# Twelve modulation tiles moved from the attention stage to later normalizations, in a two-layer hybrid decoder trunk

## The reference, cut to what matters

```
for i in range(2):
    mod = silu(c) @ ada_w[i] + ada_b[i]            # 6 sections of 1024
    sh_a, sc_a, g_a, sh_f, sc_f, g_f = split(mod, 6)
    h = rmsnorm(x, norm_mix[i]) * (1 + sc_a) + sh_a
    y = diff_attention(h) if i == 0 else retention(h)
    x = x + g_a * y
    h = rmsnorm(x, norm_ffn[i]) * (1 + sc_f) + sh_f
    x = x + g_f * moe(h)                           # 64 experts, 8 of them for a token
out = rmsnorm(x, final_norm)
```

## Time and profile before

| | us |
|---|---|
| median of 3 runs | 1436.48 (1433.49 to 1436.8) |
| the profiled execution | 1434.63 |
| its span, first to last instruction | 1432.9 |

### The profile page before, as it was taken

The page is one execution under the profiler, slowest core; times in us unless marked ns, Lnnn a source line. Parts: engine busy times, 40 slices in busy tenths (PEclk is TensorE's granted clock), DMA queues, the critical chain, the costliest instruction groups (busy, mean ns, idle before and its releaser), DMA issues.

```text
span 1432.9 us, 32974 instructions
## 1 busy us (share of the span) xinstructions
PE 1327.3 (93%) x12029; PEld 876.8 (61%) x12030; DVE 550.7 (38%) x1226; ACT 446.3 (31%) x885; POOL 207.0 (14%) x663
## 2 busy tenths in 40 slices
PE   4999789999999999998799999799999999999996
PEld 2878566555555555554499998665555555555553
DVE  2556565332223323232533455553332323322333
ACT  3443452222222222221444454522222222222222
POOL 8200102111111111111000000011111111111110
PEclk9999999999999999999899999899999999999998
DMA  9999995999999999999995434449999999999994
GB/s 352 350 382 398 407 368 209 422 420 422 421 422 423 421 421 422 423 421 421 377 290 185 168 118 147 162 175 421 421 421 421 422 421 422 422 422 421 422 422 199
DMA packets 113338, 516.06 MB, mean 360 GB/s; under 512 B 9632, under 2 KB 46624, under 8 KB 63360
## 3 DMA queue, kind: packets, MB, share of 16 engines
q1 hardware_dynamic: 109920, 509.64, 88.8%
q0 software_dynamic: 2656, 3.49, 0.9%
q10 hardware_dynamic: 704, 2.10, 0.4%
HBM read 514.10 MB, written 1.09 MB: 360 GB/s over the span
## 4 chain that ended last, share of the span: by engine, by line
PE 71%; DMA 9%; DVE 5%; SPq 5%; ACT 5%; issue 3%; POOL 1%; ACTq 1%; DVEq 0%; POOLq 0%
PE bank L933 18%; PE bank L1115 15%; PE bank L1118 8%; PE bank L1136 8%; PE bank L1050 6%; DMA ring<-in_exp_w_dram 6%; PE bank L1091 5%; PE bank L1142 4%; SPq L346 3%; DMA ring<-in_da_w_in_dram 2%; PE bank L908 2%; DVE arena L1573 1%; ACT arena L711 1%; PE bank L1125 1%; SPq L349 1%
## 5 line engine op out<-in xcount | busy, mean ns | idle before, releaser
L1115 PE MATMUL bank<-ring,arena 128*64 128x512 f32 x768 | 176.9, 600 | 11.4 <-DMA ring<-in_exp_w_dram 11.4
L1091 PEld LDWEIGHTS bank<-arena 128*128 128x128 bf16 x3264 | 142.1, 98 | 55.5 <-issue 55.0
L1050 PE MATMUL bank<-arena_r 128*128 128x512 f32 x560 | 161.3, 418 | 3.0 <-DVE arena_r L1585 3.0
L1585 DVE TENSOR_TENSOR arena_r<-bank,arena_r 128x512 fp32r<-128x512 f32 x136 | 94.1, 692 | 154.1 <-ACT arena_r L723 154.1
L1091 PE MATMUL bank<-arena 128*128 128x64 bf16 (+1 forms) x3264 | 151.8, 207 | 0.0
L716 ACT ACTIVATE arena<-bank 128x256 f32<-128x256 f32 (+1 forms) x68 | 22.6, 333 | 387.3 <-PE bank L1115 270.1
L723 ACT CAST arena_r<-bank 128x512 fp32r<-128x512 f32 x136 | 79.7, 586 | 189.4 <-PE bank L1136 124.8
L1050 PEld LDWEIGHTS bank<-arena_r 128*128 128x128 f32 x560 | 94.6, 188 | 60.2 <-issue 47.4
L542 POOL TENSOR_TENSOR arena<-arena,pass_base 128x2 f32 x136 | 23.6, 197 | 741.6 <-PE bank L1102 727.6
L933 PE MATMUL bank<-HH_r,ring_r 128*128 128x256 f32 x448 | 128.4, 287 | 0.0
L1115 PEld LDWEIGHTS bank<-ring,arena 128*64 128x64 f32 x768 | 56.0, 138 | 111.7 <-issue 111.1
(11 more groups left out here) (273 smaller groups left out, 2154.9 us busy)
## 6 DMA issues: line engine op xcount, KB each, us to landing
ring<-in_exp_w_dram SPq DMA_DIRECT2D x264, 1024.0 KB, 23.9
ring<-in_ada_w_dram SPq DMA_DIRECT2D x48, 1024.0 KB, 13.3
HH<-in_exp_w_dram SPq DMA_DIRECT2D x40, 1024.0 KB, 20.4
mods<-in_exp_w_dram SPq DMA_DIRECT2D x40, 1024.0 KB, 24.3
arena<-in_exp_w_dram SPq DMA_DIRECT2D x40, 1024.0 KB, 25.0
ring<-in_ret_w_in_dram SPq DMA_DIRECT2D x24, 1024.0 KB, 11.9
ring<-in_da_w_in_dram SPq DMA_DIRECT2D x12, 1024.0 KB, 17.2
ring<-in_ret_w_out_dram SPq DMA_DIRECT2D x8, 1024.0 KB, 4.9
```

The costliest lines, as they stand in the source:

```text
L1050: ins = nc.tensor.matmul(banks[4 + NH * tc + hf][:, :], S[:, P * tc:P * tc + P], y[:, r, 512 * hf:512 * hf + 512], start=False, stop=(last ...
L1091: ins = nc.tensor.matmul(banks[2 - 2 * half][:, P * kk:P * kk + 2 * W], parts[:, tc, r, P * (4 * half + kk):P * (4 * half + kk + 1)], Pg[: ...
L1115: ins = nc.tensor.matmul(banks[1][W * i:W * i + W, :], xg[:, k, W * i:W * i + W], w13[j][:, k, :, :], start=(k == 0), stop=(k == KD - 1))
L1585: nc.vector.tensor_tensor(y[:, 1, 512 * hf:512 * hf + 512], banks[hf][:, :], y[:, 0, 512 * hf:512 * hf + 512], ALU.subtract).then_inc(u[f" ...
```

## The change

Sections (1, 2), (1, 3) and (1, 5) are no longer made in the attention stage, which keeps three of its six in the loop and three in its tail. (1, 2) and (1, 3) are made between the first expert loop and the second layer's first transposes, (1, 5) during its second normalization; their bias rows are loaded to other places, later. The root is taken per block of tokens, with mean and epsilon in its scale and bias. Shared tile 0 is rounded before the last output tile's wait. The first two quarters of the turned heads are evicted and rounded before output tile 1 is.

The core of the diff (left out: places of rows in memory, semaphore names, counts that follow from the order, and places of the same edits on the fourth engine):

```
-LATER = [(0, 2), (0, 3), (0, 4)] + [(1, s) for s in range(6)] + [(0, 5)]
+LATER = [(0, 2), (0, 3), (0, 4), (1, 0), (1, 1), (1, 4), (0, 5), (1, 2), (1, 3), (1, 5)]
     for i in range(12):
         order.append(("mix_in", 0, i))
-        if i >= 3 and i % 3 < 2:
-            order += later[2 * (i // 3) - 2 + i % 3]
-    order += sum(later[6:9], [])
-    order += [("mix_out", 0, i) for i in range(4)] + later[9]
+        if i >= 3 and i % 3 == 0:
+            order += later[i // 3 - 1]
+    order += sum(later[3:6], [])
+    order += [("mix_out", 0, i) for i in range(4)] + later[6]
...
     order += [("expert", 0, i) for i in range(132)]
-    order += [("mix_in", 1, i) for i in range(24)] + [("mix_out", 1, i) for i in range(8)]
+    order += later[7] + later[8]
+    order += [("mix_in", 1, i) for i in range(24)] + [("mix_out", 1, i) for i in range(8)] + later[9]

 (GpSimd)
-            store_rows(1, 0, 6, 9)
-            pool.wait_ge(rows_stored, 128)
+            store_rows(1, 0, 2, 5)
+            store_rows(1, 4, 1, 6)
+            pool.wait_ge(rows_stored, 192)
...
             for l in range(DEPTH):
+                if l == 1:
+                    store_rows(1, 5, 1, 10)
+                    pool.wait_ge(rows_stored, 384)
+                    spread(1, 5, gates_in)
...
                 if l == 0:
+                    pool.wait_ge(routed_done, 2)
+                    (four loads of the bias rows of (1, 2) and (1, 3))
                     pool.wait_ge(x_new, 4)
+                    (four loads of the bias rows of (1, 5))
+                    store_rows(1, 2, 2, 9)
+                    pool.wait_ge(rows_stored, 320)
+                    turn_mods(1, 3)
                     spread(1, 2, gate1_in)

 (ScalarE, norm_stats)
                     nc.scalar.activation(h[:, tc, :], X[:, tc, :], ACT.Square, accum_out=ss[:, tc:tc + 1]
                                          ).then_inc(sumsq, 1)
-                act.wait_ge(meansq, n + 1)
-                nc.scalar.activation(rs[:, 0:TC], ss[:, 0:TC], ACT.Sqrt).then_inc(root, 1)
+                    act.wait_ge(sumsq, TC * n + tc + 1)
+                    nc.scalar.activation(rs[:, tc:tc + 1], ss[:, tc:tc + 1], ACT.Sqrt, scale=1.0 / D, bias=eps[:, 0:1]).then_inc(root, 1)

 (ScalarE, the attention stage's tail)
             round_w("mix_out", 0, 0)
             evict_aT(15)
-            release_ada(8)
+            evict_oT(0)
+            round_oT(0)
+            release_ada(5)
             square_o(14)
+            evict_oT(1)
+            round_oT(1)
+            square_o(15)
             round_w("mix_out", 0, 1)
-            for m in range(3):
-                evict_oT(m)
-            square_o(15)
-            for m in range(3):
-                round_oT(m)
+            evict_oT(2)
+            round_oT(2)
...
-            for i in range(2, 4):
-                mixer_out(0, i)
+            mixer_out(0, 2)
+            round_w("shared", 0, 0)
+            mixer_out(0, 3)
             moe(0)
             round_w("mix_in", 1, 0)
             norm_stats()
+            release_ada(7)
+            release_ada(8)
             evict_hT()
...
+            load_root_table()
+            round_w("shared", 1, 0)
+            mixer_out(1, 7)
             moe(1)

 (TensorE)
             def moe(l):
-                if l == 0:
-                    pe.wait_ge(x_new, 1)
-                    ada(*LATER[9], ada_bank[9][:, 0:256])
+                k = (6, 9)[l]
+                pe.wait_ge(x_new, 4 * l + 1)
+                ada(*LATER[k], ada_bank[k][:, 0:256])
                 turn_h()
...
             for part in range(3):
                 ...
-                later(2 * part)
+                later(part)
                 first_half(i + 1)
                 attend(n + 1)
                 second_half(i + 1)
                 turn_a(n + 2)
-                later(2 * part + 1)
                 first_half(i + 2)
...
             moe(0)
+            ada(*LATER[7], ada_bank[7][:, 0:256])
+            pe.wait_ge(x_new, 3)
+            ada(*LATER[8], ada_bank[8][:, 0:256])
+            pe.wait_ge(bank_rows_read, 8)
             turn_h()
+            pe.wait_ge(bank_rows_read, 9)

 (VectorE)
             def norm_root(last=False):
                 n = norms[0]
-                dve.wait_ge(sumsq, TC * (n + 1))
-                nc.vector.tensor_scalar(ss[:, 0:TC], ss[:, 0:TC], 1.0 / D, EPS, ALU.mult, ALU.add).then_inc(meansq, 1)
-                dve.wait_ge(root, n + 1)
-                step(nc.vector.reciprocal(rs[:, 0:TC], rs[:, 0:TC]))
-
-                if not last:
-                    for tc in range(TC):
+                for tc in range(TC):
+                    if n == 2 and tc == 1:
+                        later_rows(7)
+                    dve.wait_ge(root, TC * n + tc + 1)
+                    step(nc.vector.reciprocal(rs[:, tc:tc + 1], rs[:, tc:tc + 1]))
+                    (block tc of h, or of the output in the last normalization)
...
             low_part("mix_out", 0, 0)
+            low_oT(0)
             keep_o(15)
+            low_oT(1)
             mean_squares(last_heads, DA_ITEMS)
-            for m in range(3):
-                low_oT(m)
+            low_oT(2)
...
             norm_root()
+            later_rows(8)
             low_part("mix_in", 1, 0)
             evict_hT()
```

More of the change, by code:

```diff
@@ L305, in trunk @@
             turns.append(("proj", i))
-            if i % 3 < 2:
-                turns.append(("ada", 2 * (i // 3) - 2 + i % 3))
-        turns += [("ada", k) for k in range(6, 9)]
+            if i % 3 == 0:
+                turns.append(("ada", i // 3 - 1))
+        turns += [("ada", k) for k in range(3, 6)]
         proj0_bank = {i: banks[7 * (n % 2)] for n, (kind, i) in enumerate(turns) if kind == "proj"}
@@ L467, in store_rows @@
                 pool.wait_ge(rows_ready, ready)
-                rows = browB[:, first:first + count, :] if l == 1 else row5 if first == 5 else browA[:, first - 2:first - 2 + count, :]
+                rows = (browA if (l, first) == (0, 2) else row5 if (l, first) == (0, 5) else rows23 if (l, first) == (1, 2)
+                        else row5_1 if (l, first) == (1, 5) else browB[:, first:first + count, :])
                 for q in range(4):
@@ L664, in round_rw @@
                 act.wait_ge(late_consts_in, 16 * 5)
-                act.wait_ge(rows_stored, 128)
+                act.wait_ge(rows_stored, 192)
                 nc.scalar.copy(rw_hi, rw[:, :, :]).then_inc(rw_rounded, 1)
             def moe(l):
-                if l == 1:
-                    load_root_table()
-                round_w("shared", l, 0)
                 norm_stats()
@@ L779, in _ @@
                 square_o(n)
-                release_ada(2 * part)
+                release_ada(part)
                 evict_proj0(i + 2)
@@ L783, in _ @@
                 square_o(n + 1)
-                release_ada(2 * part + 1)
                 evict_aT(n + 3)
@@ L841, in evict_proj1 @@
                 elif i < 8:
+                    if i == 4:
+                        act.wait_ge(rows_stored, 320)
                     evict_proj(kT[:, 2 * (i - 4):2 * (i - 4) + 2, :])
@@ L886, in _ @@
             round_yT(3)
-            for i in range(2, 8):
+            for i in range(2, 7):
                 mixer_out(1, i)
@@ L1250, in _ @@
             scores(14)
-            later(6)
+            later(3)
             attend(12)
@@ L1254, in _ @@
             scores(15)
-            later(7)
+            later(4)
             attend(13)
             turn_a(14)
-            later(8)
+            later(5)
             attend(14)
@@ L1676, in _ @@
                 finish_a(n + 2)
-                later_rows(2 * part)
+                later_rows(part)
                 keep_o(n + 1)
@@ L1681, in _ @@
                     low_part("mix_in", 0, i + 2)
-                later_rows(2 * part + 1)
                 keep_o(n + 2)
@@ L1801, in _ @@
             moe(1)
+            dve.wait_ge(last_gain, 16)
             norm_root(last=True)
-            dve.wait_ge(last_gain, 16)
-            for tc in range(TC):
-                nc.vector.scalar_tensor_tensor(out=h[:, tc, :], in0=X[:, tc, :], scalar=rs[:, tc:tc + 1], in1=gains[:, 4, :],
-                                               op0=ALU.mult, op1=ALU.mult).then_inc(h_ready, 1)
 _INS = ["x", "c", "norm_mix", "norm_ffn", "ada_w", "ada_b", "da_w_in", "da_w_out", "da_lq1", "da_lk1", "da_lq2",
```

89 lines of the change are left out of this document (54 added, 35 removed).

## The result

The changed kernel takes 1442.16 us (median of 5 runs, 1439.49 to 1443.35), the kernel before beside it 1435.74 (5 runs, 1433.49 to 1436.8). The ratio is 1.0046, with a 95% interval of 1.0032 to 1.006: slower, by 6.4 us, where 1431.5 was forecast. It lies outside of the range, by 1.2 us. The profiled execution took 1439.49, the shortest of the five, with a span of 1437.8 against 1432.9.

The account below looks back on a forecast made before the run. Bounds differ by stretch: full transfer engines in the first expert loop, TensorE's instruction stream in the attention stage. Terms -17.0 - 1.1 + 17.0 - 2.5 - 1.4 = -5.0 us, from median 1436.48 to 1431.5; range 1422 to 1441.

Parts of the forecast that it names:

- The step that failed: Both expert loops: only their starts move, since the same instructions free what feeds them; 0 us change in length.
- Attention stage and tail: Start to output projection's end: three sections of 3.6 gone, ScalarE waits gone, 1.0 back at `turn_a`, tail 4.7; 17.0 us sooner.
- the tail: Output projection: tiles land sooner relative to TensorE, `mix_out(0)` starts 4.6 sooner, 4.8 from `mix_out(1)`; 4.7 taken, bounds 0 to 6.4.
- First layer's second normalization: Cast of shared tile 0 leaves the stretch and blocks are normalized separately; 1.1 us sooner, bounds 0.4 to 1.6.
- Boundary: Between the layers: eight modulation tiles delay the first retention tile, and ScalarE's queue behind it; costs 17.0 us, bounds 1.5 to 20.
- Second layer: Its second normalization: shared tile 0's cast and table load leave, one section is added; 2.5 us sooner, bounds 1.4 to 2.5.
- the lower bound: Second layer's second normalization: gain of only 1.4 us, if the added section delays the transposes.
- End: Last normalization: block 0 is written while block 1 is squared; 1.4 us sooner, 1.0 if the engines wait for each other.
- Rival 1: Attention stage: its chain of waits replaces the removed sections, stage gives 7.2 us, sum +4.8, 1441 us; chance 0.13.
- The rival that transfers bound the attention stage: Attention stage: twelve tiles fewer at 2.56 us give 30.7 us, sum -18.7, 1418 us; chance 0.05.

Follow-up runs that it names:

- 28 instructions of filler: Changed kernel plus 28 instructions of already-met semaphore waits in TensorE's program ahead of the first expert loop: 1429.79 us, ratio 0.9963.
- the loop that begins at 177: Second loop, 177 instructions into a 256-instruction block; changed kernel plus 112 instructions of already-met waits ahead of the first loop: 1478.12 us.
- 141: Second loop's start within a 256-instruction block; changed kernel with two sections moved instead of three, plus 76 instructions of already-met waits: 1432.38 us.
- 156: Second loop's start within a block; changed kernel with two sections moved instead of three, plus 91 instructions of already-met waits: 1459.22 us.
- 166: First loop's start within a block, in the changed kernel (1442.16 us) and in the kernel before plus 125 instructions of already-met waits (1507.27 us).
- 168: First loop's start within a block; changed kernel with only section (1, 5) moved, none at the boundary, no added waits: 1442.28 us.
- 190: Second loop's start within a block; kernel before plus 125 instructions of already-met waits ahead of the first loop, no work moved: 1507.27 us.

## Why the prediction was wrong, by its own steps

**The step that failed** is in its sum: "Both expert loops only move with their starts: what feeds them is freed by the same instructions as before." That speaks of what is fed by tiles. A loop is also fed by its instructions, and of those the change moved 387 from ahead of the loop to behind it. The body that had touched seven blocks of 16384 bytes touched eight, and was loaded anew at each return. The runs show it from both sides: moved to a good place the changed body costs nothing, and the old body, moved to a bad one, costs 72 us in the two loops. The Trainium skill (Runtime: NRT & Kernel Launch, Instruction fetch mechanics) gives TensorE 128 KiB for instructions, filled in blocks of 16 KiB, and says that a taken branch to a block that isn't held waits for a transfer. The traces agree with it: 16384 bytes a packet, 216 ns when all is held and 6 us when not. Eight such blocks would make up the 128 KiB, but with eight touched it no longer works here, only with seven. That one block is taken by what is loaded ahead is my reading; the nine packets of a stalled iteration, one more than the eight blocks that its body touches, fit it, and no run tested it. The Trainium skill (Advanced Engine Details and Errata, ISA Cache) also says that there are only two lines of 16 KiB. The trace disagrees: with two no body of 1592 instructions could return without a packet, and 44 packets in all, with clean returns, show seven held.

The rest of the sum was nearly right. With 28 instructions of filler in place of the stall, the span fell by 5.0 us, which was the forecast, and the time was 1429.8 for a forecast 1431.5. That it fits to the tenth is luck: the stage gave 2.4 us more than its term, the boundary cost 1.3 more and the second layer gave 1.0 less. The terms:

- *Attention stage and tail*, -17.0 forecast, -19.7 found. The tail's first section starts 13.8 us sooner (139.15 for 152.95), where 12.3 were counted. The waits at `turn_a` are 1.9 us in all in three places, where the sum had 2.4 + 1.0: the old one is down to 1.2, and the two new ones are under 0.4 each, so the chain did not take the sections' place. `mix_out(0)` starts 19.0 us sooner (156.65 for 175.68), so the tail gave 5.2, where 4.6 were counted. The last 0.7 the clock gave, which no step of the sum had. Busy time and granted clock (the last value but two) of the first output projection and of the rest, before and after:

```profile
175.70:182.90 7.20, 7.20 (x26) 5.80 (x27) 4.08 (x6) 0.25 (x2) 1.46 (x3) 0.78 1.03 387
182.90:200.30 17.40, 17.07 (x76) 13.51 (x74) 8.84 (x7) 5.96 (x5) 0.00 (x0) 1.00 0.98 400
```

```profile
156.60:162.90 6.30, 6.17 (x28) 4.92 (x28) 3.50 (x7) 3.97 (x8) 2.00 (x3) 1.00 1.03 411
164.00:180.60 16.60, 16.60 (x73) 13.40 (x73) 8.83 (x7) 6.38 (x6) 0.00 (x0) 1.00 1.02 414
```

  Before, TensorE had waited 4.9 us ahead of the first one and ran part of it at the 1.2 GHz level; now it had waited 1.7 and ran at full clock. Both stretches together are 22.8 us busy for 24.3. Of this 1.5, 0.8 went again in waits (1.1 us for the second tile's low part, where 0.3 had been idle).
- *First layer's second normalization*, -1.1 forecast, -1.9 found (-1.0 where filler stands in it), 0.3 past the bound of 1.6. The routing's first product comes 1.2 sooner behind the section (211.35 - 200.31 = 11.0 before, 190.43 - 180.60 = 9.8 after); the other 0.7 lie behind it, in the routing, and their cause stays open.
- *Boundary*, +17.0 forecast, +18.3 found without the stall. The first retention tile landed at 700.0, 18.2 us behind the loop's end (16.6 forecast), and from there to the projection it was 12.5 us (12.7 forecast). From the last expert tile's landing to the retention tile's it was 24.9 us, and 3.0 before: 21.9 for eight tiles, where 20.5 was counted. Seven of them landed 2.4 to 2.8 us apart, one 3.9. In the changed kernel itself it was +8.1, since in 36.5 us of pauses the transfers got ahead; the tile came 7.9 us behind the loop's end. The stall thus cost 22.0 in the loop and gave 10.3 back behind it.
- *Second layer*, -2.5 forecast, -1.5 to -1.7 found. The normalization itself gave the 2.5: the first eviction begins 7.3 us behind the last output product and not 9.9, and the section is not what delays the transposes, as the lower bound had it. It ends 0.3 before them, and they wait for VectorE's block:

```profile
925.94 3.66 PE L933 MATMUL bank<-ring,cb 128*32 128x256 f32 x64
...
929.88 1.09 PE L945 MATMUL bank<-ident,HH 128*128 128x128 f32 x8 [0.28 <-DVE HH L1452]
...
933.26 1.00 ACT L629 ACTIVATE mods<-bank,mod_T 128x256 f32<-128x256 f32 x2
```

  1.0 us was lost behind it, in the routing's first 24 products. TensorE waits 3.2 us right ahead of them, where it was 1.4, and they run at the 1.2 GHz level for longer (before, then after):

```profile
930.10:934.70 4.60, 4.55 (x24) 4.31 (x24) 4.60 (x6) 2.59 (x5) 0.00 (x0) 0.66 0.00 0
```

```profile
935.80:941.40 5.60, 5.58 (x24) 5.22 (x24) 5.08 (x7) 2.52 (x5) 0.18 (x1) 0.52 1.00 420
```

- *End*, -1.4 forecast, -1.5 found.

Rival 1 named 1441 us, which is near to the result, but its mechanism did not occur: the stage gave more than forecast, not 7.2. No rival held a cost in a loop of which no line changes. The rival that transfers bound the attention stage falls with the 19.7 (it wanted 30.7).

What would have shown it ahead of time was in the kernel before: the row of the instruction queue with only 8 packets in 463 us of a loop whose body is six blocks and a quarter, and the short branch records. They say that the body is held as a whole, and so that it can stop being held.

## What to carry to other kernels

When a change moves instructions from one side of a long loop to the other, count the blocks of code that the body touches before and after, as one counts bytes in a buffer; the packets of the instruction queue and the length of the branch at the loop's end show at once which case a kernel is in. A result that a small shift of code can turn by 25 us says nothing of the edit that was timed: compare with both bodies held before judging the parts. And price a section of work at each place by what is the bound there: in the attention stage a section cost 3.7 to 4.5 us, about what TensorE works on it (3.6), at the boundary 9 to 11, about what its four tiles take to land (10.2, an estimate from 2.56 each), though TensorE idles there.

## What the runs showed of the hardware that was not expected

- A return to a body of seven blocks takes 216 to 239 ns and no packet; with eight, the branch takes 6.0 to 7.0 us, and a second pause of 2.3 to 4.2 us follows where, by the count, the body's first block ends (one pause of 10.4 to 10.9 us where it begins at a block's last instructions). The products behind run at the 1.2 GHz level of the clock. It is 12.4 us in all, four times in the loop that begins at 177. The weights' transfers ran at full rate beside them (408 to 418 GB/s around the first slow return of the loops that begin at 141, 156, 166, 168, 177 and 190), so what a return costs beside idle transfers stays open.
- The transition isn't sharp: with up to 14 instructions in the eighth block one return of four was slow, with 18 to 21 three (one run each), from 28 on all.
- A pause of TensorE is not lost altogether where transfers are the bound: 24.5 us around waits for tiles went away in it, and 10.3 us came back at the boundary; in the loop without such waits all of it was lost.
